# Loads of the last stage's gate rows and final norm weights, moved from the GpSimd queue to the sync queue

## The reference

```python
    h = modulate(rmsnorm(x, g_ffn), sh2, sc2)
    x = x + gt2 * moe_ffn(h, w_rg, b_rg, w_re, b_re, w_eg, w_eu, w_ed)
    ...
y_prompt = rmsnorm(xp, g_final)
y_sample = rmsnorm(xs, g_final)
```

## Time and profile before

| | us |
|---|---|
| median of 3 runs | 1836.56 |
| the runs | 1833.71, 1836.56, 1844.71 |
| the profiled execution's own time | 1837.52 |
| its span in the trace | 1835.9 |

### The profile page before, as it was taken

The page is one execution under the profiler, slowest core; times in us unless marked ns, Lnnn a source line. Parts: engine busy times, 40 slices in busy tenths (PEclk is TensorE's granted clock), DMA queues, the critical chain, the costliest instruction groups (busy, mean ns, idle before and its releaser), DMA issues. The chain is left out here.

```text
span 1835.9 us, 21665 instructions
## 1 busy us (share of the span) xinstructions
PE 1576.8 (86%) x8893; PEld 815.0 (44%) x8893; DVE 398.2 (22%) x878; ACT 198.7 (11%) x521; POOL 166.1 (9%) x360
## 2 busy tenths in 40 slices
PE   5999999999999999977888778888888787777774
PEld 2455454444454444555445343434444444443431
DVE  2012322224242320452111101010101010101117
ACT  3001111111211100110000000000000000000003
POOL 1031000000102020020101010101010100000100
PEclk9999999999999999979999999999999999999997
DMA  9998777656626594379999999999999999999992
GB/s 364 382 308 302 286 272 298 266 218 261 201 69 240 175 243 140 160 268 418 423 427 427 428 426 427 427 427 425 426 426 423 426 424 426 423 425 422 420 399 100
DMA packets 103622, 617.25 MB, mean 336 GB/s; under 512 B 15701, under 2 KB 17861, under 8 KB 67977
## 3 DMA queue, kind: packets, MB, share of 16 engines
q1 hardware_dynamic: 85922, 571.73, 76.8%
q0 software_dynamic: 17648, 44.79, 7.9%
HBM read 603.03 MB, written 34.16 MB: 347 GB/s over the span
## 5 line engine op out<-in xcount | busy, mean ns | idle before, releaser
L1298 PE MATMUL bank<-ring,zbuf 128*64 128x256 f32 x4096 | 463.6, 382 | 89.5 <-DMA ring<-in_w_expert_up 81.8
L1298 PEld LDWEIGHTS bank<-ring,zbuf 128*64 128x64 f32 x4096 | 291.8, 138 | 269.2 <-DMA ring<-in_w_expert_up 104.8
L1321 PE MATMUL bank<-ring,hbuf 128*64 128x512 f32 x1024 | 260.9, 668 | 16.8 <-ACT hbuf L1672 16.8
L861 PE MATMUL bank<-ring,hbuf 128*128 128x512 f32 x384 | 174.2, 599 | 2.9 <-ACT xbuf L1443 2.6
L1321 PEld LDWEIGHTS bank<-ring,hbuf 128*64 128x64 f32 x1024 | 80.2, 153 | 176.6 <-issue 174.3
L857 PE MATMUL bank<-hbuf,ring 128*128 128x384 f32 x384 | 133.8, 495 | 1.2 <-ACT zbuf L1439 0.8
L1161 PE MATMUL bank<-ring,zbuf 128*128 128x512 f32 x288 | 128.7, 602 | 3.1 <-DVE ring L1982 1.8
L2159 DVE TENSOR_SCALAR hbuf<-hbuf 128x256 f32<-128x256 f32 x32 | 9.4, 294 | 527.1 <-ACT hbuf L1642 527.1
L861 PEld LDWEIGHTS bank<-ring,hbuf 128*128 128x128 f32 x384 | 70.2, 190 | 83.6 <-issue 82.6
L857 PEld LDWEIGHTS bank<-hbuf,ring 128*128 128x128 f32 x384 | 69.8, 190 | 52.5 <-issue 11.0
L1161 PEld LDWEIGHTS bank<-ring,zbuf 128*128 128x128 f32 x288 | 54.3, 192 | 69.9 <-issue 69.8
(11 more groups left out here) (408 smaller groups left out, 1153.2 us busy)
## 6 DMA issues: line engine op xcount, KB each, us to landing
ring<-in_w_expert_up SPq DMA_DIRECT2D x64, 2048.0 KB, 26.8
ring<-in_w_expert_gate SPq DMA_DIRECT2D x64, 2048.0 KB, 25.6
ring<-in_w_expert_down SPq DMA_DIRECT2D x64, 2048.0 KB, 23.2
ring<-in_w_ada SPq DMA_DIRECT2D x96, 1024.0 KB, 8.1
ring<-in_w_in SPq DMA_DIRECT2D x32, 1024.0 KB, 9.3
ring<-in_w_out SPq DMA_DIRECT2D x16, 1024.0 KB, 5.2
y_rows<-modr POOLq DMA_DIRECT2D x1, 6144.0 KB, 22.5
ring<-y_rows SPq DMA_DIRECT2D x3, 2048.0 KB, 20.0
```

What stands on the lines that cost most here:

```text
L861: last = mm(bank[t][:, :], hT[:, k, t * P:(t + 1) * P], w[:, kk_, :], start=(k == 0), stop=(k == KC - 1))
L1298: last = mm(bank[2 + u][64 * q:64 * q + 64, 256 * (j // 4):256 * (j // 4) + 256], xeT[u][:, k % 8, k // 8, :], w[:, kk_, 256 * q:256 * q + ...
L1321: last = mm(bank[5 + n][64 * q:64 * q + 64, :], hidT[u][:, k % 2, k // 2, :], unit(8 + k)[:, 1024 * q + QN * n:1024 * q + QN * n + QN], st ...
```

## The change

POOL no longer issues the eleven gate loads and the load of `g_final`. SP issues them, behind the last weights of expert 31: the two `gate_half` loads before `rows_back(0)`, the prompt's gate row between `rows_back(0)` and `rows_back(1)`, the eight sample rows and `g_final` after `rows_back(2)`. The eight sample rows have a semaphore of their own (`gbs_in`); DVE waits for it ahead of the last stage's `add_late(0)`, and its wait ahead of `early_sum(0)` covers the two `gate_half` loads and the prompt's row only.

```diff
+            sp.wait_ge(mod_out, 64)
+            for q in range(2):
+                sp.dma_start(gate_half[64 * q:64 * q + 64, :],
+                             mod_dram[3, 0:1, 1024 * q:1024 * q + 1024].broadcast_to([64, 1024])).then_inc(gbc_in, 16)
             for t in range(NT):
                 sp.wait_ge(unit_used, U_MOE + UE * (NE - 1) + 2 * t + 2)
                 if t == 0:
                     sp.wait_ge(sct[0], 16 * 16)
                     sp.wait_ge(sct[1], 16 * 15)
                 rows_back(t)
+                if t == 0:
+                    sp.dma_start(gbc[:, 0, :], mod_dram[3, 0:1].broadcast_to([P, D])).then_inc(gbc_in, 16)
+            for b in range(DEC_B):
+                sp.dma_start(gbc[DEC_T * b:DEC_T * b + DEC_T, 1, :],
+                             mod_dram[3, b + 1:b + 2].broadcast_to([DEC_T, D])).then_inc(gbs_in, 16)
+            sp.dma_start(gfin, A["g_final"].unsqueeze(0).broadcast_to([P, D])).then_inc(gfin_in, 16)
...
-            spread_rows(gbc[:, 0, :], gbc[:, 1, :], 3, gbc_in)
-            for q in range(2):
-                g.dma_start(gate_half[64 * q:64 * q + 64, :],
-                            mod_dram[3, 0:1, 1024 * q:1024 * q + 1024].broadcast_to([64, 1024])).then_inc(gbc_in, 16)
-            pool.wait_ge(x1, 6)
-            g.dma_start(gfin, A["g_final"].unsqueeze(0).broadcast_to([P, D])).then_inc(gfin_in, 16)
...
-                        dve.wait_ge(gbc_in, 176)
+                        dve.wait_ge(gbc_in, 48)
...
                 early_add(1)
                 dve.wait_ge(early, 2)
+                dve.wait_ge(gbs_in, 16 * DEC_B)
                 with dve.Fori(0, n_over) as i:
...
             fin.n = 8
+            dve.wait_ge(gbs_in, 16 * DEC_B)
             dve.wait_ge(gfin_in, 16)
```

More of the change, by code:

```diff
@@ L284, in encoder_step @@
         osq, r_exp, og_sb, ogT_ps, ogT_sb = sem("osq"), sem("r_exp"), sem("og_sb"), sem("ogT_ps"), sem("ogT_sb")
-        mod_out, gate_in, norm_in, gbc_in, ffn_in = (sem(n) for n in ("mod_out", "gate_in", "norm_in", "gbc_in", "ffn_in"))
+        mod_out, gate_in, norm_in, gbc_in, gbs_in, ffn_in = (sem(n) for n in ("mod_out", "gate_in", "norm_in", "gbc_in", "gbs_in", "ffn_in"))
         x1, x1sq, x1sum = sem("x1"), sem("x1sq"), sem("x1sum")
```

## The result

| | before | after |
|---|---|---|
| median, us (10 runs each) | 1835.44 | 1842.63 |
| lowest and highest | 1831.79, 1844.71 | 1840.59, 1847.35 |
| the profiled execution's own time | 1837.52 | 1842.76 |
| its span | 1835.9 | 1841.2 |

The ratio is 1.0040, with an interval of 1.0028 to 1.0052: the change costs 7.2 us. That is slower, though within 1%, and just outside my range. The forecast of 1834.2 was 8.4 us too low. As a change it missed by 9.6 us (+7.2 measured, -2.4 forecast), because the median of the kernel before came out 1.1 us lower here than the one I started from.

A forecast was written before the change was run, and what follows sets the result against it. The DMA stream, full from expert 1 through the row loads, was taken as the bound. Terms -4.4 + 1.2 + 0.3 + 0.5 = -2.4 us, from a median of 1836.56, gave 1834.2 us; range 1830.5 to 1842.

The forecast's parts named there:

- What bounds the kernel: Expert 1 to the row loads: late DMA engines work without a gap, so the end moves with yk[0]'s landing and DVE.
- the 2.3 us that I gave as a lower bound of the gain: End of expert 0: PE's own gain from the earlier second gather, if the weight stream gained nothing; 2.3 us.
- Gain 4.4: Expert 1's first gate half lands after 7.6 us, not 12.0, once the early loads are gone: 4.4 us gained.
- `gate_half` ahead of `yk[0]`, 1.2: Behind the last weights: gate_half's bytes, a quarter of a row load, delay yk[0] by 1.2 us; 2.7 at 197 GB/s.
- The prompt's gate row, 0.3: Behind yk[0]: DVE waits for this row ahead of early_sum(0), costing 0.3 us, at most 3.2.
- The sample rows and `g_final`, 0.5: DVE waits for both ahead of add_late(0): landing takes 17.55 us against 17.07 available, costing 0.5 us, at most 3.4.
- SP's issues at 0.3 to 0.5 us each: In the tail: SP's twelve more issues run while the queue is 10 us behind, so they cost nothing.
- DVE's waits become the bound: Rival, ahead of early_sum(0) and add_late(0): all spread rows move at 197 GB/s, +4.9 us, 1841.5; chance 0.2.
- The loads were hidden: Rival, before expert 1: moving the loads gains only 0.3 us or loses 2.0, 1836.3 to 1838.6; chance 0.2.
- the two that I named as proof of error: Wrong if expert 31's weights come no earlier, or if one of DVE's two waits is over 2 us.

The follow-up runs named there:

- no_loads: The changed kernel with all twelve loads left out and the three tiles cleared by POOL, so outputs using them are wrong; median 1831.72, ratio 0.9983.
- gather_first: The kernel before with only the second gather issued ahead of the twelve loads; 1835.25, ratio 0.9998.
- late_wait_moved: The changed kernel with DVE's wait for the gate row behind early_sum(0), not ahead of it; median 1844.45, ratio 1.0039.
- late_one_load: late_distinct with the eight sample loads made one load of 128 partitions and the two gate_half loads one; median 1834.88, ratio 0.9988.
- late_waits_late: The changed kernel with DVE's waits for gate row, sample rows and g_final put where the data are first read; median 1840.55, ratio 1.0032.
- early_strided: The kernel before, loads in the old place, reading different w_out rows, sample and gate_half loads writing every eighth and every second partition; median 1832.8, ratio 0.9989.
- early_wide: The kernel before, second gather first, then four whole-width loads on POOL, sample rows and gate_half from rows spread out in DRAM beforehand; 1833.4, ratio 0.9985.
- late_distinct: The changed kernel with the twelve loads reading as many different w_out rows as partitions, not one spread row, into the same partitions; median 1842.84, ratio 1.0041.
- late_strided: late_distinct with only the partitions changed: sample loads write every eighth partition, gate_half loads every second; median 1835.24, ratio 1.0004.
- late_wide: The changed kernel with sample rows and gate_half spread out in DRAM at about 592 us, each then one load of 128 partitions; 1834.88, ratio 0.9993.
- late_no_half: The changed kernel with only the two gate_half loads back on POOL, ahead of the second gather; median 1839.6, ratio 1.0021.
- all_early: The kernel before, SP issuing g_final and gate_half between expert 0's gate and down weights, POOL the rest behind the second gather; 1836.45, ratio 1.0003.
- half_copied: gather_first with g_final issued by SP behind expert 0's weights and gate_half copied on the chip by POOL; 1836.99, ratio 1.0001.
- half_copied_strided: half_copied with the sample rows loaded by 16 loads of 8 partitions that lie 16 apart; 1835.61, ratio 0.9999.

## Why the prediction was wrong, step by step

All three profiles on one scale, from gate(1), in us:

| | before | `no_loads` | after | forecast for after |
|---|---|---|---|---|
| `yk[0]` ready (ACT) | 963.8 | 960.0 | 966.5 | 960.6 |
| from there to `add_late(0)` | 19.2 | 19.2 | 23.7 | 20.0 |
| `add_late(0)` | 983.0 | 979.2 | 990.2 | 980.6 |

The forecast column is the one of before, less 4.4 and plus 1.2 at `yk[0]`, then plus 0.8. The error of 9.6 us is 0.6 in the gain, 5.3 in `gate_half` and 3.7 in the terms behind `yk[0]`.

- **What bounds the kernel: right.** The DMA stream is full from expert 1 to the row loads, and bytes out of it are worth their time. `gather_first` shows no worth in PE's wait alone (ratio 0.9998 [0.9989, 1.0007]), so the 2.3 us that I gave as a lower bound of the gain were none. That some DMA engines rest while others are 10 us behind stays my reading; no run tests it.
- **Gain 4.4: right in kind, a little large.** The first gate half landed at 7.9 (forecast 7.6), `down` at 838.59 where I had 841.6 (839.6 on the shifted scale), a us earlier than I said. The fourth half of expert 1 lands 23.4 from gate(1) (829.89 + 3.79 - 0.33 + 13.2 = 846.5) where it was 26.7, so the stream is 3.3 ahead, not 4.4. `no_loads` gives 3.8 in its profile and 3.1 by its ratio.
- **`gate_half` ahead of `yk[0]`, 1.2: this is the step that failed.** It cost 6.5 us. I took the full rate for the 64-partition loads, on the ground that `g_final`, a 128-partition load, had moved beside weights at 426 GB/s. That row spoke of 128 partitions only. On every second or on all 128 partitions the same bytes cost `yk[0]` 0.8 to 2.8 us (960.9 to 962.8 against 960.0), and my 1.2 lies in that. And I counted only the loads' own bytes. They also slow what moves beside them: the last weights land 958.5 from gate(1) against 955.0 in `no_loads`, and `yk[0]` 8.0 us after those instead of 5.0. That is the 3.5 and the 3.0 of the 6.5.
- **The prompt's gate row, 0.3: about right, and not what is paid.** It landed 5.0 us after `yk[0]` in the changed kernel's profile (DVE began 5.0 after `yk[0]`, 2.12 before), which is near the upper bound of 3.2. But with the same loads it was 2.7 and 2.5 us in two other profiles, and `late_wait_moved` shows that this wait is hidden in the one for `g_final`.
- **The sample rows and `g_final`, 0.5: too small, the second step that failed.** DVE waited 1.52 us at L2245. `g_final` landed 23.6 us after `yk[0]` where my terms had 20.0 (2.45 and 17.55), and DVE began `add_late(0)` 4.5 us later behind `yk[0]` than before, not 0.8. In `late_wait_moved` it was 3.5.
- **SP's issues at 0.3 to 0.5 us each: wrong, at no price that I can show.** The eight sample issues took 13.04 us, and `g_final` was issued only at 1782.3. It landed 31 us later, so it was far behind in the queue all the same; the one sample load of `late_one_load` took 5.86 us to issue at the same place, and that kernel was not slower than before.
- **The rivals.** "DVE's waits become the bound" (1841.5, chance 0.2) had the slow rate, part of the place and nearly the time, and the time in part by luck: it gave `gate_half` 2.7 us where 6.5 were paid, and the two waits 6.6 where 4.5 were. Moving the waits (`late_waits_late`) brought 2 us at most. It spoke of slowness only as a matter of the spread row, and it left out that the weights beside it slow down. "The loads were hidden" is wrong for the loads as they were, since `no_loads` gains 3.1 us; but `early_strided` and `early_wide` keep them early in another shape and get 2.0 and 2.8 of that.
- **The signs to watch.** Of the two that I named as proof of error, the first did not occur (expert 31's last weights were issued 5.4 us earlier from gate(1)); the second, a DVE wait over 2 us, did, at the gate row. And `yk[0]`, which I had landing 3.2 us earlier, landed 2.7 later from gate(1). The 1% that I took for the least that a measurement can tell was too wide: the interval of the ratio reaches 0.12% to either side.

My reading of the earlier trace rows was the root. The 197 GB/s stood there with a share of 0.98; I put them down to spread rows on which all 16 engines were at once, and asked nothing about the partitions. Late in the kernel `late_distinct` against `late_strided` puts the low rate down to the partitions written, and early `early_wide` moves the same bytes at 415 GB/s.

The Trainium skill ("SBUF — State Buffer", section "Door 1: The DMA port swizzle") says that DMA bandwidth depends on how many of the 16 SBUF ports the written partitions reach, with a map by bits of the partition number. By that map 16 neighbours reach 4 ports, 64 neighbours 8, every second partition all 16 and every eighth 8. This case agrees for `gate_half`: 267 GB/s with 64 neighbours beside the weights, 418 with every second partition, 420 to 425 on all 128 (`late_one_load`, `late_wide`, 1776 to 1782). For the sample rows a step from 4 ports to 8 hardly shows: 220 GB/s with 16 neighbours (`late_no_half`) and 229 with every eighth partition (`late_strided`), 412 on all 128. The rows show besides that the weights beside the narrow `gate_half` loads land 3.5 us later.

## What to carry to other kernels

Ask of every small load how many partitions it writes and what moves beside it: 0.5 MB on two groups of 64 neighbours made the next load land 6.5 us later behind a full weight stream, the same bytes on spread or on all 128 partitions 0.8 to 2.8 us. A DMA share of 1.0 is not a rate. Here every stretch with a full share and about half the usual GB/s held loads to few partitions. Look for such a load there, and mend its shape (one whole-width load from a DRAM copy laid out in advance) before you move it.

## What the runs showed of the hardware

- In stretches with loads that write 16 or 64 neighbouring partitions the DMA engines showed a share of 1.0 and 197 to 267 GB/s. The last 2048 KB weight load beside `gate_half` lost with them: 28.3 us to landing instead of 23.2 in `no_loads`. Of these 5.1 us 1.6 are an earlier issue, and 3.5 a later landing from gate(1).
- Reading one DRAM row for all partitions is not slow by itself: 415 GB/s in `early_wide`, and `late_distinct` with distinct rows was no faster than the change (1842.84 against 1842.63). Up to 2 us of the change may still be due to it; the runs leave that open.
- An issue on SP can take far longer than 0.4 us when many loads are still under way: 7.45 us for the first of the eight sample loads (chain of waits of the changed kernel). That a full queue holds it is my reading; no run shows the queue:

```profile
1769.22 7.45 SPq L473
1776.71 0.84 SPq L473
```

- With new bytes ahead of the first gather or beside it PE waited 1.7 to 3.5 us longer for it (8.84 to 10.65 us, 7.15 before), and a gain of 4 us in the landing of the first gate half did not show in the time (`all_early`, `half_copied`, `half_copied_strided`).
